# Expert weights of an MoE layer: the first four tiles of w_up get two places each, and TensorE and SyncE loop over two experts in a turn

## The reference

```python
logits = (xf @ w_router + b_router)
top_val, top_idx = lax.top_k(logits, 4)          # 4 of 32 experts for each token
top_w = jax.nn.softmax(top_val, axis=-1)
...
hu = x_pad[toks] @ w_up[e] + b_up[e]             # w_up[e]: 1024 x 2048
ys = clamped_swiglu(hu) @ w_down[e] + b_down[e]  # w_down[e]: 1024 x 1024
```

## Time and profile before

| | |
|---|---|
| median of 3 executions | 1398.05 us (1396.36 to 1400.24) |
| the profiled execution's own time | 1392.76 us |
| span of the profiled execution | 1391.0 us |
| TensorE busy | 1186.3 us (85%) |
| VectorE, ScalarE busy | 309.0 us, 253.2 us |
| bytes moved by DMA | 464.79 MB, 334 GB/s over the span |
| mean granted TensorE clock | 0.938 |

### The profile page before, as it was taken

How to read it: one execution, slowest core, us unless ns; L and a number is a source line. 1 busy time by engine, 2 the same in 40 slices (tenths; PEclk the granted TensorE clock), 3 DMA queues, 4 the chain that set the end, 5 groups by cost and what they waited for, 6 DMA issues and landing times.

```text
span 1391.0 us, 20661 instructions
## 1 busy us (share of the span) xinstructions
PE 1186.3 (85%) x7931; PEld 582.3 (42%) x7932; DVE 309.0 (22%) x783; ACT 253.2 (18%) x370; POOL 0.2 (0%) x4
## 2 busy tenths in 40 slices
PE   4999899987977899998678777877787889799996
PEld 2745588835332334243234332333333333434432
DVE  1125454264111122121112111111111112103213
ACT  3035422112012111112111112111112020200211
POOL 0000000000000000000000000000000000000000
PEclk9999999997999999999899889987899999799998
DMA  9942475353779999989999999999999999955890
GB/s 335 380 154 90 177 262 212 137 213 152 278 267 419 416 417 418 418 356 420 418 416 417 418 418 418 418 418 416 417 419 418 418 418 417 415 198 181 337 415 34
DMA packets 102361, 464.79 MB, mean 334 GB/s; under 512 B 8124, under 2 KB 9364, under 8 KB 69430
## 3 DMA queue, kind: packets, MB, share of 16 engines
q1 hardware_dynamic: 100368, 461.52, 83.1%
q10 hardware_dynamic: 1958, 2.78, 0.6%
HBM read 463.22 MB, written 1.05 MB: 334 GB/s over the span
## 4 chain that ended last, share of the span: by engine, by line
PE 39%; DMA 19%; SPq 13%; issue 3%; DVE 2%; ACT 0%; DVEq 0%
PE psum L876 17%; DMA ring<-in_w_up 14%; PE psum L949 10%; SPq L485 7%; PE psum L826 6%; SPq L480 6%; DMA ring<-in_w_down 5%; PE psum L868 2%; PE psum L967 2%; DVE area L1540 1%; PE psum L912 1%; PE psum L851 1%; DVE area L1525 1%; PE psum L817 0%; DVE area L1563 0%
## 5 line engine op out<-in xcount | busy, mean ns | idle before, releaser
L876 PE MATMUL psum<-ring,area 128*32 128x512 f32 (+2 forms) x2432 | 413.1, 649 | 77.1 <-DMA ring<-in_w_up 77.0
L876 PEld LDWEIGHTS psum<-ring,area 128*32 128x32 f32 (+2 forms) x2432 | 101.9, 123 | 375.7 <-issue 227.6
L949 PE MATMUL psum<-ring,area 128*32 128x256 f32 (+1 forms) x2080 | 199.0, 422 | 26.5 <-DVE area L1525 14.8
L826 PEld LDWEIGHTS psum<-area 128*128 128x128 f32 x1056 | 131.4, 206 | 35.1 <-issue 35.1
L826 PE MATMUL psum<-area 128*128 128x128 f32 x1056 | 138.0, 292 | 0.3 <-DVE area L1470 0.3
L949 PEld LDWEIGHTS psum<-ring,area 128*32 128x32 f32 (+1 forms) x2080 | 71.7, 114 | 143.2 <-issue 79.6
L1500 DVE TENSOR_SCALAR area<-psum 128x256 f32<-128x256 f32 x51 | 21.6, 424 | 453.8 <-PE psum L876 453.8
L1138 ACT ACTIVATE area<-area 128x256 f32<-128x256 f32 x51 | 21.3, 417 | 443.3 <-DVE area L1500 443.3
L1126 ACT ACT_TABLE_LOAD x32 | 41.1, 1283 | 327.8 <-PE psum L851 327.8
L525 PE MATMUL psum<-hT,ring 128*128 128x256 f32 x370 | 83.6, 386 | 0.0
L525 PE MATMUL psum<-ring,hT 128*128 128x512 f32 (+1 forms) x192 | 77.8, 561 | 0.0
(11 more groups left out here) (177 smaller groups left out, 666.4 us busy)
## 6 DMA issues: line engine op xcount, KB each, us to landing
ring<-in_w_up SPq DMA_DIRECT2D x256, 1024.0 KB, 19.3
ring<-in_w_down SPq DMA_DIRECT2D x128, 1024.0 KB, 22.7
ring<-in_ada_w SPq DMA_DIRECT2D x12, 2048.0 KB, 16.6
ring<-in_w_in SPq DMA_DIRECT2D x11, 2048.0 KB, 19.6
ring<-in_w_out SPq DMA_DIRECT2D x2, 2048.0 KB, 10.2
ring<-in_w_branch_b SPq DMA_DIRECT2D x1, 2048.0 KB, 9.6
cst<-in_cst ACTq DMA_DIRECT2D x1, 1168.0 KB, 9.4
x_res<-in_x SPq DMA_DIRECT2D x1, 1024.0 KB, 5.1
```

The source lines that it names most:

```text
L826: ins = pe.matmul(ps[banks[i]][:, kk % 4 * P:(kk % 4 + 1) * P], h2[:, tt, kk * P:(kk + 1) * P], S[:, tt, 0:P], start=(tt == 0 and kk % 4 = ...
L876: ins = pe.matmul(ps[b][g * P // G:(g + 1) * P // G, 0:w], XT[:, kk, t0:t0 + P // G], wt[:, c0:c0 + w], start=False, stop=kk == KT - 1, sk ...
L949: ins = pe.matmul(ps[b][g * M:(g + 1) * M, 0:w], hidT[:, p, q * P + of * M:q * P + (of + 1) * M], down_weights(kk)[:, g * W + d * CW:g * W ...
```

## The change

Each of the first four tiles of w_up gets a second place, for the odd experts: in `hT`, in `arena[:, 0:2048]`, in `xn`, and in a buffer that holds `ybT` and `b_down` together. The other eight tiles keep their one place in the ring. The semaphores are one for each tile and parity. The four tiles of expert `e` may be loaded once expert `e-2` has used them. Since the addresses now depend on whether an expert is even or odd, SyncE's loop and TensorE's loop hold two experts in a turn, so that TensorE's program has all seven bodies twice (`pe0_*` and `pe1_*`). Expert 1 is loaded ahead of the loop, its tile 0 when `hb11` is full, its tile 3 when `acc_done` has risen. `kept` moves to the masks in `cst`, to `arena` and to `silu_router`. VectorE and ScalarE still loop over one expert.

```diff
+TILES, TWICE, AROUND = 12, 4, 2
-        def up_weights(kk):
-            return slot(NF + kk // 2)[:, kk % 2 * 2 * F:(kk % 2 + 1) * 2 * F]
+        def place(j, i):
+            return TILES + i if j % 2 and i < TWICE else i
+        def tile(j, i):
+            n = place(j, i)
+            if n < TILES:
+                return slot(NF + n // 2)[:, n % 2 * 2 * D:(n % 2 + 1) * 2 * D]
+            return (hT[:, :], arena[:, 0:2 * D], xn, ybT_b_down[:, :])[n - TILES]
...
-        def experts(eng, tag, one):
+        def experts(eng, tag, one, each=1):
...
+                e = nc.snap(i, min_val=0, max_val=E - each)
+                rest = []
+                for j in range(each):
+                    rest += one(e + j if j else e, j, root)
+                nc.regs_add(i, i, each)
...
+            def freed(e, i):
+                if i < TWICE:
+                    return up_used, (KT - 2) * (e - 2) + i + 1
+                if i < KT - 2:
+                    return up_used, (KT - 2) * (e - 1) + i + 1
+                if i < KT:
+                    return up_full, MAX_U * e
+                if i < TILES - 1:
+                    return dn_used, 3 * (e - 1) + i - KT + 1
+                return dn_full, MAX_D * e
...
-                    pe.wait_ge(up_tile[kk], 16 * e + 16)
+                    arrived_tile(kk)
...
-            experts(pe, "pe", lambda e, root: [by_class(pe, pe.value_load(cls_i[0:1, ds(e, 1)]), lambda k: body(e, k), "pe", root)])
+            experts(pe, "pe", lambda e, j, root: [by_class(pe, pe.value_load(cls_i[0:1, ds(e, 1)]), lambda k: body(e, j, k),
+                                                 f"pe{j}", root)], AROUND)
```

More of the change, by code:

```diff
@@ L306, in layer_kernel @@
         ld_gain = [sem("ld_gain1"), sem("ld_gain2")]
-        up_tile = [sem(f"up_tile{i}") for i in range(KT)]
-        dn_tile = [sem(f"dn_tile{i}") for i in range(FT // 2)]
+        tile_in = [[sem(f"tile_in{h}_{i}") for i in range(TILES)] for h in range(2)]
         up_used, dn_used = sem("up_used"), sem("dn_used")
@@ L476, in _ @@
                 sp.dma_start(chunk(g, width, kt), src).then_inc(slot_full[g % RING], 16)
[L478 to L507, removed]
+            def load(e, j, i):
+                if i < KT:
+                    src = a["w_up"][0][ds(e, 1), i * P:(i + 1) * P, :]
+                    sp.dma_start(tile(j, i), src.rearrange("e p n -> p (e n)")).then_inc(tile_in[j % 2][i], 16)
+                else:
+                    src = a["w_down"][0][ds(e, 1), (i - KT) * 2 * P:(i - KT + 1) * 2 * P, :]
+                    sp.dma_start(tile(j, i).rearrange("p (k n) -> p k n", k=2),
+                                 src.rearrange("e (k p) n -> p (e k) n", p=P)).then_inc(tile_in[j % 2][i], 16)
@@ new lines, in freed @@
+            def freed(e, i):
[3 more added lines that the diff above has]
+                    return up_used, (KT - 2) * (e - 1) + i + 1
+                if i < KT:
+                    return up_full, MAX_U * e
+                if i < TILES - 1:
+                    return dn_used, 3 * (e - 1) + i - KT + 1
+                return dn_full, MAX_D * e
+            for i in range(TILES):
+                if i % 2 == 0:
+                    sp.wait_ge(*released[names[NF + i // 2 - RING]])
+                load(0, 0, i)
@@ new lines, in _ @@
+            for e in range(1, AROUND):
+                for i in range(TILES):
+                    if e == 1 and i == 0:
+                        b, n = un.place["hb11"]
+                        sp.wait_ge(bank_full[b], n + 1)
+                    elif e == 1 and i == 3:
+                        sp.wait_ge(acc_done, 1)
+                    elif e > 1 or i > 3:
+                        sp.wait_ge(*freed(e, i))
+                    load(e, e, i)
+            only = [sp.engine]
+            n = nc.alloc_registers("sp_i", engines=only)
@@ new lines, in _ @@
+            nc.regs_mov(n, AROUND)
+            nc.br("sp_loop", engines=only)
+            with nc.body("sp_loop", valid_engines=only):
+                e0 = nc.snap(n, min_val=AROUND, max_val=E - AROUND)
+                for j in range(AROUND):
+                    e = e0 + j if j else e0
+                    for i in range(TILES):
+                        sp.wait_ge(*freed(e, i))
+                        load(e, j, i)
+                nc.regs_add(n, n, AROUND)
+                nc.br_lt(n, E, "sp_loop", "sp_end", engines=only)
@@ L508, in _ @@
+            nc.switch_bb("sp_end")
             for tt in range(TT):
@@ L1133, in body @@
                     for j in range(SPILLED[k]):
-                        ins = act.activation(kept[:, j, :], ps[3 - j], ACT.Copy)
+                        ins = act.activation(kept[j], ps[3 - j], ACT.Copy)
                     ins.then_inc(spilled, 1)
@@ L1531, in body @@
                 for j in range(SPILLED[k]):
-                    ins = v.tensor_copy(ps[3 - j], kept[:, j, :])
+                    ins = v.tensor_copy(ps[3 - j], kept[j])
                 if SPILLED[k]:
@@ L1541, in body, with expert @@
                         at += 1
-            def expert(e, root):
+            def expert(e, j, root):
                 cls = v.value_load(cls_i[0:1, ds(e, 1)])
```

37 lines of the change are left out of this document (21 added, 16 removed).

## The result

The changed kernel takes 1464.34 us (median of 4 runs, 1462.56 to 1468.88), the one before 1397.20 us (4 runs, 1394.06 to 1400.24). The ratio is 1.0486, with a 95% interval of 1.0451 to 1.052. It is slower, as forecast, but by 67 us and not by 12, and outside the range.

A forecast was written before the change was run, and what follows sets the result against it. Transfers bound experts 10 to 25, TensorE 4 to 9 and 28 to 31. Lead left -2.8, end stalls +15.6, longer existing gap -0.6: +12.2 us on the 1398.05 us median, so 1410 us; 8-in-10 range 1386 to 1430.

The forecast's parts named there:

- Second places: Four tiles issued ahead into an empty queue: 6.6 us earlier at expert 3, 10 us from expert 10 on.
- the lead absorbs part of the lateness: At expert 9's tiles: despite +3.8 us up to expert 8, the stream from expert 10 on is still earlier.
- the stream is 2.8 us earlier: From expert 10 through 28: tile 4 of expert 9 issued at 624.0 us, where it was moved from 626.8.
- Code must be fetched: TensorE's doubled bodies, 11.5 to 14.5 packets, exceed the 5.7 to 8.8 that stay, so fetches return, 5.2 us a stall.
- five in the open: Stalls before experts 7, 8, 29, 30 and 31 that no wait for tiles hides, 5.2 us each, 26 us together.
- Code that follows in sequence comes ahead of its use: TensorE's instruction fetch: only branches to code not held stall; the front's 11 packets came without such gaps.
- those at 2, 17 and 18 are hidden: Stalls before these three experts are covered by 70.8 us of tile waits; uncovered they would add 15.6 us.
- (c): Rival: bodies crowd each other out nearly every turn, 12 experts stall, 62 us less 10, up to 1449 us; chance 0.13.
- both class 0 bodies together are 3.3 packets and stay: Argument against stalls at nearly every turn: 752 records stay held between two runs of a big class.
- (a): Rival, faster: code is held better, at most one of five open stalls real; 1390 or 1388 us; chance 0.23.
- (d): Rival: SyncE is held at tile 4 as before at tile 0, leaving stalls alone, +10 to +25 us; chance 0.03.
- Gaps of 10 us and more: Sign that would prove the forecast wrong: longer "issue" gaps, if a fetch waits behind a deeper queue of tiles.

## Why the prediction was right in sign and wrong in size

**Second places: right.** The 6.6 us at expert 3 and 10 us from expert 10 on were measured as 6.7 and 10.9 us in the run with the steps twice. With class 0 alone, where the queue is empty only once, the places gave 6.8 us of the 11.0. The mechanism, four tiles issued into an empty queue, shows in the window at 391 to 400 us. That the lead absorbs part of the lateness was right too: in the full change 41.1 us at expert 8 became 34.7 at expert 10, while with one place for every tile 36.7 stayed 36.8. The step "the stream is 2.8 us earlier" failed only because the lateness put into it was +3.8 us and was +41.1.

**Code must be fetched: right, and all of the loss.** Doubling the bodies alone gives 1464.59 us, and each late expert comes with packets on q8. The signs forecast were there: packets of q8 in the loop (29; 68 on the page, I had said 50), and "issue" gaps at 7, 8, 17, 18, 29, 30 and 31.

**The term that was mis-sized: "five in the open" x 5.2 us.** It stood for 26 us and measured 79.5 us, at eight experts. Both factors were too small: eleven stalls at 5.2 us would be 57 us, and the price makes up the rest.
- Count: eleven stalls in the open, not five. Experts 4, 6 and 27 were not on my list, and 7, 8 and 31 had two. Expert 6 was the first of class 1; before, it began after 0.89 us, and I had not asked whether its code would still come ahead once other bodies lay in between. I stepped through the experts with eight packets held, some 230 records in each, the top of the bounds. The runs show that counting records of what runs is too kind: two class 2 bodies are 1256 records, 5.5 packets by that count, fewer than the 1320 records that stayed before, and yet the run with class 2 alone fetched 81 packets in 780 us, that is 13 for each pair of experts (127.6 us); and 1384 records of classes 0 and 1 lost something three times. Code of other bodies also comes without being run: in the kernel before no packet began between 390.9 and 1204.9 us, and yet class 1 first ran at 535.00 us, in expert 6, so its code had been read before. That such code crowds out other code is argued, not shown.
- Price: I took 4.3 to 6.1 us from two gaps, and 5.2 as the mean. The 4.3 came from a gap with the queue nearly empty, and of the stalls in the open only the second wait before expert 8 met a queue that had run empty. The first wait at experts 4, 6, 7, 27, 29, 30 and 31 was 5.1 to 6.2 us longer than the gap there before. What my price left out is the clock: it was 0.50 behind a stall, and the bias took 1.93 us for 1.07, the steps on w_up of expert 2 8.1 us for 7.1. Together a single stall cost 7.2 to 8.9 us.
- "Code that follows in sequence comes ahead of its use" fails right behind a branch: 4.55 us at expert 7 and 4.25 us at 31 lie inside a body, after three transposes.
- Cover: "those at 2, 17 and 18 are hidden" holds for 17 and 18. The earlier trace rows begin at 618 us and say nothing of expert 2. There the stall was hidden only in part: expert 3 ended 3.9 us earlier than before and not 6.7, though it waited for no tile of w_up.

For the first of these points, the first instruction of class 1 in the kernel before:

```profile
535.00 0.43 PE L851 MATMUL psum<-cst,area 128*128 128x128 f32 x2 [0.89 <-issue]
```

With the measured terms the sum closes: up to expert 8 two experts with one stall (8.9 and 8.7 us) and two with two (13.1 and 14.6 us) add 45.3 us to the -3.9 us at expert 3, and expert 5 takes 0.3 us back, which is the 41.1 us measured; the transfers take back 3.6 us up to 26; experts 27 to 31 add 7.8 + 0.2 + 7.2 + 7.6 + 11.6 = 34.4 us. That is 71.9 us, of the 72.3 between the two profiled executions.

**What hid the others.** Experts 2 (in part), 14, 17 and 18 stalled, and their time went into waits for tiles: the total for w_up from 420 to 1200 us fell from 77.0 to 45.0 us, while transfers kept 417 GB/s from 662 us on.

**The rivals.** (c), nearly every turn stalls, was the nearest: eight of its twelve experts did. It had 0.13, and its 1449 us (1398 + 62 - 10 is 1450) were too low for want of the second wait and of the clock, though it let all twelve stall. I set it aside by a count of records: "both class 0 bodies together are 3.3 packets and stay" holds by itself, as the class 0 pair shows, but says nothing of what a class 2 body between them drops. (a) falls: at most one real stall in the open was its condition. (d) falls by the lead measured. "Gaps of 10 us and more", named as a sign against me, came at expert 8. Packets of q8 began at 642.3, 647.8, 648.4 and 652.7 us in that gap (639.9 to 653.5 us), so these are waits one after the other, of some 6 to 7 us each. The run with class 2 alone has such pairs at nearly every expert. But the guess behind that sign was not empty: at expert 1 the same stall took 6.40 us behind a queue that moved 427 GB/s and 4.59 us behind one that was nearly empty. So the filled hole itself made that stall 1.8 us longer; 10 us it made of none.

The Trainium skill, "Runtime: NRT & Kernel Launch", section "Instruction fetch mechanics", was right against this change in that a taken branch to code that isn't held waits for a fetch. Its statement that only two blocks are held, which it works out for a memory of 32 KiB, does not hold for TensorE here: with class 0 alone 752 records, 3.3 packets, went round without one packet on q8 from 420 to 1200 us. Of its figures for TensorE it is the eight blocks of 16 KiB that fall inside my bounds of 5.7 to 8.8 packets; its 2048 instructions are more than the 2020 records of the upper bound.

**Open.** In what order code is dropped; why 1256 or 1384 doubled records don't stay where 1320 did, and whether code that comes ahead and isn't run is the reason; whether bodies that pick the place of a tile by a register, without code twice, would keep the 10.9 us. That was not tried.

## What to carry to other kernels

A loop unrolled by two, in which each turn branches to one of several big bodies, doubles the code that must stay near the engine. Before such a change look at the instruction queue's packets in the loop: where there are none now, and the code that goes round nears what a rare big body already crowds out, each return can cost 7 to 9 us of an engine's time. Count packets and not only the records that run, and price a stall with what the lower clock behind it costs. Vary an address with the least code in it, here the four steps and not the body, and ask which resource, transfer or engine, is bound at each place of a stall: the same gap was free at expert 17 and cost 7 us and more at 27.

## What the runs showed of the hardware that I had not expected

- Behind about 6 us without work TensorE's granted clock was 0.50, though it had been busy before; the work that followed was up to 1.8 times as long (1.93 against 1.07 us).
- A branch to code that isn't held can wait twice: 12.2 to 15.0 us at experts 4 to 30 of the run with class 2 alone, 13.68 us at expert 8, or 5.93 and then 4.55 us three transposes later.
- A fetch starts later behind data. When expert 1 was reached with the data queue at 427 GB/s, the packet on q8 began 2.4 us after TensorE's last work, and TensorE waited 6.40 us; with it nearly empty (65 GB/s) it began after 0.7 us, and TensorE waited 4.59 us.
- How much code goes round doesn't decide alone. 1320 records stayed for 780 us in the kernel before, 1256 in two bodies were fetched anew at every expert.
